# A hybrid decoder's step: products for 64 sample rows put on both column halves of TensorE's array, and cached keys taken from two samples in turn

## The reference, cut to what matters

```python
cq, ckv, kr, dq, dk, dv, iq, iw, ik = jnp.split(xn @ w_in, offs, axis=-1)   # 1024 x 1768
...
s = (jnp.einsum('bthc,bsc->bhts', ql, ckv).astype(jnp.float32)
     + jnp.einsum('bthr,bsr->bhts', qr, kr).astype(jnp.float32)) * scale    # MLA scores
...
s = jnp.einsum('btgnd,btkgd->btgnk', qg, kg).astype(jnp.float32) * DSA_HEAD_DIM ** -0.5
...
return jnp.concatenate([o_mla, o_dsa.reshape(b, t, DSA_HEADS * DSA_HEAD_DIM)], axis=-1) @ w_o
...
return jnp.einsum('bhtm,bmhd->bthd', p, v).reshape(b, t, X_HEADS * X_HEAD_DIM) @ wo_x
```

## Time and profile before

| | |
|---|---|
| median of 3 runs | 2436.02 us (2435.57 to 2438.84) |
| profiled execution, whole | 2440.92 us |
| profiled execution, span from first to last instruction | 2439.2 us |
| PE busy | 2232.2 us (92%) |
| DVE, POOL, ACT busy | 1606.9, 1041.5, 882.3 us |
| mean granted TensorE clock | 0.927 |

### The profile page before, as it was taken

One profiled execution on the slowest core, in us unless ns is written; L12 is line 12 of the kernel. 1 busy time (PEld: TensorE's weight loads), 2 busy tenths in 40 slices (PEclk: granted clock), 3 DMA queues, 4 the chain that ended last, 5 costly groups with the idle time before them and its releaser, 6 DMA issues.

```text
span 2439.2 us, 37526 instructions
## 1 busy us (share of the span) xinstructions
PE 2232.2 (92%) x12808; PEld 1809.7 (74%) x12808; DVE 1606.9 (66%) x3389; ACT 882.3 (36%) x1407; POOL 1041.5 (43%) x968
## 2 busy tenths in 40 slices
PE   6988789899778969969999995999999999999998
PEld 3534445366674549969999995888888888888886
DVE  1333986187112336888899982688878888888775
ACT  2115234122122222245555562343334333343343
POOL 1001003442110012207877725787878777773221
PEclk9988679899878669989999997999999999999999
DMA  5000001545434024148888877499998989999983
GB/s 194 10 9 18 1 4 49 155 138 166 132 139 164 1 90 163 44 147 231 221 227 241 235 239 263 161 327 357 341 357 319 342 323 349 330 327 332 327 281 116
DMA packets 240121, 479.95 MB, mean 197 GB/s; under 512 B 49249, under 2 KB 141794, under 8 KB 238562
## 3 DMA queue, kind: packets, MB, share of 16 engines
q1 hardware_dynamic: 161666, 314.60, 38.2%
q0 software_dynamic: 71680, 144.69, 18.3%
q10 hardware_dynamic: 6624, 18.88, 2.2%
HBM read 436.26 MB, written 41.80 MB: 196 GB/s over the span
## 4 chain that ended last, share of the span: by engine, by line
PE 51%; DVE 3%; DMA 2%; ACT 1%; issue 0%; POOL 0%; SPq 0%; POOLq 0%; ACTq 0%
PE psC L2216 30%; PE psC L2233 19%; PE psC L2204 2%; DMA rU<-in_peer_uT 1%; DVE Ul L2042 1%; ACT Uh L1962 0%; DVE gi L1392 0%; DMA gates<-gst 0%; DVE ohC L2058 0%; DVE gv L1389 0%; DVE cand L1396 0%; DVE wide L1455 0%; DVE ohI L2055 0%; SPq L1850 0%; POOL stD L1949 0%
## 5 line engine op out<-in xcount | busy, mean ns | idle before, releaser
L2216 PE MATMUL psC<-xh,Uh 128*128 128x256 f32 (+1 forms) x2048 | 611.5, 299 | 44.8 <-DVE Ul L2042 42.9
L2216 PE MATMUL psC<-xl,Uh 128*128 128x256 f32 (+1 forms) x2048 | 605.9, 296 | 0.0
L2216 PE MATMUL psC<-xh,Ul 128*128 128x256 f32 (+1 forms) x2048 | 605.4, 296 | 0.0
L2216 PEld LDWEIGHTS psC<-xh,Uh 128*128 128x128 f32 x2048 | 387.4, 189 | 57.8 <-issue 25.5
L1911 POOL DMA_INDIRECT ring<-in_peer_v,idxV x256 | 293.8, 1148 | 246.9 <-DVE h L2099 133.8
L2216 PEld LDWEIGHTS psC<-xh,Ul 128*128 128x128 f32 x2048 | 387.9, 189 | 5.8
L2216 PEld LDWEIGHTS psC<-xl,Uh 128*128 128x128 f32 x2048 | 387.3, 189 | 0.0
L2042 DVE TENSOR_TENSOR Ul<-rU,Uh 128x1024 fp32r<-128x1024 f32 x256 | 312.2, 1221 | 89.8 <-ACT Uh L1962 88.6
L1919 POOL DMA_INDIRECT aS<-acts,idxA x256 | 313.7, 1225 | 79.6 <-issue 77.7
L2099 DVE SCALAR_TENSOR_TENSOR h<-ring,wS,h 128x1024 f32<-128x1024 f32 x256 | 327.7, 1287 | 10.4 <-DMA ring<-in_peer_v,idxV 10.1
L1962 ACT ACTIVATE Uh<-rU 128x1024 fp32r<-128x1024 f32 x256 | 270.0, 1055 | 131.1 <-DMA rU<-in_peer_uT 128.2
(11 more groups left out here) (305 smaller groups left out, 3341.7 us busy)
## 6 DMA issues: line engine op xcount, KB each, us to landing
rU<-in_peer_uT SPq DMA_DIRECT2D x256, 512.0 KB, 5.1
rV<-in_peer_v SPq DMA_DIRECT2D x128, 512.0 KB, 5.4
gr<-gates SPq DMA_DIRECT2D x32, 640.0 KB, 7.6
arena<-in_poolM SPq DMA_DIRECT2D x128, 128.0 KB, 2.1
acts<-stage SPq DMA_DIRECT2D x32, 512.0 KB, 5.3
gates<-gst ACTq DMA_DIRECT2D x6, 2048.0 KB, 8.5
wraw<-in_w_pq SPq DMA_DIRECT2D x16, 512.0 KB, 3.5
gates<-zeros SPq DMA_DIRECT2D x4, 2048.0 KB, 8.8
```

What stands on the lines that cost most here:

```text
L2216: last = M(bank(6 + k, hi - lo), a[:, at, c], x[:, d, lo:hi], start=(d == 0 and a is Uh and x is xh), stop=(d == KD - 1 and x is xl))
```

## The change

Four products change, and nothing else.

1. For the 64 sample rows, the projection takes the ranges 0 and 1 together and then 2 and 3: for every `k`, one `M` for the even range into partitions 0 to 63 of its bank and one for the odd range into partitions 64 to 127 of its bank. Before the first `M` of a pair, PE waits until both banks of the block before are copied out.
2. `pair_scores` takes a page of sample 0 and a page of sample 1 in turn, where it took four pages of one and then four of the other.
3. W_o of the samples alternates the two column halves, the second on partitions 64 to 127.
4. Cross W_o does so for the sample block, after a wait for both additions of the block before.

DVE and ACT read the upper partitions where the result is there.

```diff
+        def proj_bank(t, c):
+            return bank(2 + c, PC, p1=P) if t < 4 else bank(2 + c, PC, p0=NS * (c % 2), p1=NS * (c % 2) + NS)
+        def rows_of_half(t, half):
+            return {"p0": 0, "p1": P} if t < 4 else {"p0": NS * half, "p1": NS * half + NS}
...
-                for c in range(4):
+                for cs in ((0,), (1,), (2,), (3,)) if t < 4 else ((0, 1), (2, 3)):
                     if t >= 1:
-                        pe.wait_ge(S["pj_act"] if c < 2 else S["pj_dve"], 2 * (t - 1) + c % 2 + 1)
+                        pe.wait_ge(S["pj_act"] if cs[0] < 2 else S["pj_dve"], 2 * (t - 1) + cs[-1] % 2 + 1)
                     for k in range(KD):
-                        last = M(bank(2 + c, PC, p1=R), xT[:, k, toks(t)], win[:, k, c * PC:(c + 1) * PC],
-                                 start=(k == 0), stop=(k == KD - 1))
-                    last.then_inc(S["pj_mm"], 1)
+                        for c in cs:
+                            last = M(proj_bank(t, c), xT[:, k, toks(t)], win[:, k, c * PC:(c + 1) * PC],
+                                     start=(k == 0), stop=(k == KD - 1), skip_group_check=True)
+                            if k == KD - 1:
+                                last.then_inc(S["pj_mm"], 1)
...
                 for kc in range(5):
                     n = 512 if kc < 4 else NS
-                    for b2 in range(2):
-                        b = 2 * p + b2
...
-                        for a in range(4 if kc < 4 else 1):
+                    for a in range(4 if kc < 4 else 1):
+                        for b2 in range(2):
+                            b = 2 * p + b2
...
-            for half in range(2):
-                for k in range(KD):
-                    last = M(bank(2 + half, p1=NS), xT[:, k, SEQ:NTOK], w_o[:, k, 512 * half:512 * half + 512],
-                             start=(k == 0), stop=(k == KD - 1))
-                last.then_inc(S["wo_mm"], 1)
+            for k in range(KD):
+                for half in range(2):
+                    last = M(bank(2 + half, **rows_of_half(4, half)), xT[:, k, SEQ:NTOK],
+                             w_o[:, k, 512 * half:512 * half + 512], start=(k == 0), stop=(k == KD - 1),
+                             skip_group_check=True)
...
-            for i in range(2 * NBLK):
-                t, half = divmod(i, 2)
-                R = rows(t)
-                if i >= 2:
-                    pe.wait_ge(S["hx_done"], i - 1)
+            for t in range(NBLK):
+                for halves in ((0,), (1,)) if t < 4 else ((0, 1),):
+                    if t >= 1:
+                        pe.wait_ge(S["hx_done"], 2 * (t - 1) + halves[-1] + 1)
```

More of the change, by code:

```diff
@@ L423, in _ @@
                     act.wait_ge(S["pj_mm"], 4 * t + c + 1)
-                    nc.scalar.activation(proj[0:R, t, c * PC:(c + 1) * PC], bank(2 + c, PC, p1=R), ACT.Copy)\
+                    nc.scalar.activation(proj[0:R, t, c * PC:(c + 1) * PC], proj_bank(t, c), ACT.Copy)\
                         .then_inc(S["pj_act"], 1)
@@ L613, in _ @@
                     dve.wait_ge(S["pj_mm"], 4 * t + c + 1)
-                    V.tensor_copy(proj[0:R, t, c * PC:(c + 1) * PC], bank(2 + c, PC, p1=R))\
+                    V.tensor_copy(proj[0:R, t, c * PC:(c + 1) * PC], proj_bank(t, c))\
                         .then_inc(S["pj_dve"], 1)
@@ L890, in _ @@
                 hs = h[0:NS, 4, 512 * half:512 * half + 512]
-                V.tensor_tensor(hs, bank(2 + half, p1=NS), hs, ALU.add).then_inc(S["h_done"], 1)
+                V.tensor_tensor(hs, bank(2 + half, **rows_of_half(4, half)), hs, ALU.add).then_inc(S["h_done"], 1)
             norm_gain("mem")
@@ L911, in _ @@
                 hs = h[0:R, t, 512 * half:512 * half + 512]
-                V.tensor_tensor(hs, bank(i % 2, p1=R), hs, ALU.add).then_inc(S["hx_done"], 1)
+                V.tensor_tensor(hs, bank(i % 2, **rows_of_half(t, half)), hs, ALU.add).then_inc(S["hx_done"], 1)
             dve.wait_ge(S["hx_done"], 2 * NBLK)
@@ L1195, in pair_scores @@
                     n = 512 if kc < 4 else NS
-                    for b2 in range(2):
-                        b = 2 * p + b2
[L1198 to L1201, removed]
-                        for a in range(4 if kc < 4 else 1):
+                    for a in range(4 if kc < 4 else 1):
+                        for b2 in range(2):
+                            b = 2 * p + b2
+                            if kind == 0:
+                                q = qlTs[:, b, :, :].rearrange("p h t -> p (h t)")
+                            else:
+                                q = bdq[:, b, :, :, :].rearrange("p g n t -> p (g n t)")
                             if kc < 4:
@@ L1298, in _ @@
             pe.wait_ge(S["wo_in"], 16)
-            for half in range(2):
-                for k in range(KD):
-                    last = M(bank(2 + half, p1=NS), xT[:, k, SEQ:NTOK], w_o[:, k, 512 * half:512 * half + 512],
-                             start=(k == 0), stop=(k == KD - 1))
-                last.then_inc(S["wo_mm"], 1)
+            for k in range(KD):
[3 more added lines that the diff above has]
+                             skip_group_check=True)
+                    if k == KD - 1:
+                        last.then_inc(S["wo_mm"], 1)
             norm_transpose("mem")
@@ L1332, in _ @@
             pe.wait_ge(S["at_oe"], n_self + n_cross)
-            for i in range(2 * NBLK):
-                t, half = divmod(i, 2)
-                R = rows(t)
-                if i >= 2:
-                    pe.wait_ge(S["hx_done"], i - 1)
[L1338 to L1341, removed]
+            for t in range(NBLK):
+                for halves in ((0,), (1,)) if t < 4 else ((0, 1),):
+                    if t >= 1:
+                        pe.wait_ge(S["hx_done"], 2 * (t - 1) + halves[-1] + 1)
+                    for c in range(2):
+                        for half in halves:
+                            last = M(bank(half, **rows_of_half(t, half)), oxT[:, c, toks(t)],
+                                     wox[:, c, 512 * half:512 * half + 512], start=(c == 0), stop=(c == 1),
+                                     skip_group_check=True)
+                            if c == 1:
+                                last.then_inc(S["ox_mm"], 1)
 SELECT_SEMS = """cst_in key_in sq_done ms_done rstd_done xs_done tp_done xf_done xh_done xl_done
```

## The result

In six runs beside six of the kernel before, the changed kernel takes 2417.66 us against 2437.09: a ratio of 0.9921, 95% interval 0.9900 to 0.9943. So it is 19.4 us faster, where 23.4 were forecast; 2417.66 lies in the range given, near its upper end. Six more runs later gave 2418.12 against 2437.74. The profiled execution after has a span of 2420.3 us, 18.9 less than before.

What follows compares the result with a forecast made beforehand. TensorE, busy 92% of the 2439.2 us span, was taken as the bound. Terms 11.5 + 13.9 - 2.1 + 0.1 = 23.4 us, off the median 2436.02, gave 2412.6; range 2405 to 2420.

Steps and rivals of the forecast that it cites:

- Projection, 11.5 us: Samples' projection: 64 records become 32 slots, 12.0 us saved, less 0.48 for waiting on ACT's second copy; net 11.5.
- The first rival: All changed products: issuing in turn leaves weight loads unhidden, one before each product; 17 us slower, 2453; chance 3%.
- Pairs, 13.9 us: Cached pairs' scores: blocks of 8 slots save 0.43 us each at full clock; 13.9 in all, 10 to 16.8.
- Pairs 1 to 3, forecast 5.2: Cached scores at full clock, 0.43 us saved per block; part of the 6.9 forecast for pairs 1 to 4.
- Pairs 4 to 7, forecast 6.9: Cached scores: pair 4 at full clock; pairs 5 to 7 save 5.2 us, each beginning at 1.2 GHz.
- Pair 0, forecast 1.8 saved: First cached pair: three blocks at 1.2 GHz save 2.6 us, 0.8 given back if the clock rises when it did before.
- That just fits: Pair 3's last page: there near 577.3, PE comes at 577.9; caps the first three pairs' gain at 5.8 us.
- more than 2 us: Sign at pair 3: the forecast would be wrong if this pair waited longer than that.
- the rival in which pages hold the pairs: Pairs 5 to 7's pages land no earlier, pair 3 waits a little: 5.2 + 1.7 us not gained; 2419.5; chance 10%.
- W_o, 2.1 us lost: Samples' W_o: gain hidden by the memory cache's transfer, next product starts at half clock; 0.3 gained to 3 lost.
- W_o is felt: Rival at samples' W_o: memory cache lands sooner, W_o gives some 7 us, PE does not cool; 2403.5; chance 5%.
- Cross W_o, 0.1 us gained: Cross W_o's sample block: 1.7 us less, about 1.0 lost waiting for additions, 0.6 for DVE's last two; 0.1 left.

Runs made afterwards that it cites:

- pairs_alone: Kernel before with only the new order of the cached products (pages of sample 0 and 1 in turn); 2424.50 us, ratio 0.9950 to the kernel before.
- wo_alone: Kernel before with only W_o of the samples changed to alternate halves; 2438.84 us, ratio 1.0007 to the kernel before.
- pages_apart: Changed kernel with GpSimd's and ACT's shares of pair 4's pages issued only after pair 3's pages land; 2417.41 us, ratio 0.9920 to the kernel before.
- after_again: The changed kernel once more, unaltered, beside others on one chip; 2418.12 us, ratio 0.9910 to the kernel before.
- wo_cache: Kernel before with the samples' W_o change and a separate semaphore for the cross attention's memory cache; 2429.84 us, ratio 0.9972 to the kernel before.
- proj_alone: Kernel before with only the projection's part of the change; 2425.70 us, ratio 0.9953 to the kernel before.

## Why the forecast was right, and what it mis-sized

*Projection, 11.5 us: right.* The column falls by 10.6 to 12.4 us in the eight kernels with this part on both halves, and back with the halves taken away. The wait for ACT's second copy grew from 0.77 us to 1.20. The first rival falls: 64 records with 64 loads on all rows take 12.09 us. The rule of the Trainium skill named there (page "TensorE: Matmul & The Clock Gate", section "Part 3: Packing small matmuls": a load overlaps a matmul in flight only in another row group) does not hold here either.

*Pairs, 13.9 us: right in the block, too high in the sum.* The block saves 0.49 us (1.51 to 1.02) where I had 0.43 (1.09 left), so counting 12 and 8 slots came close. The whole time of pairs_alone, 13.6 us, is what was forecast. By places, against the one trace of the kernel before and over the nine with the new order, the gain is 10.5 us in the mean (6.0 to 13.8):
- Pairs 1 to 3, forecast 5.2: their mean is 100.7 us against 105.3, 4.6 less, with the waits in it; the traces with short waits reach 5.8.
- Pairs 4 to 7, forecast 6.9: mean 107.5 against 114.2, 6.7 less. The waits before pairs 5 and 6 stayed as I said.
- **Pair 0, forecast 1.8 saved, is the term that failed.** Its mean is 42.1 us against 41.3: nothing saved. I assumed that the clock would rise "at the same time as now"; it rose after 17.0 us in the profiled execution, where pair 0 had spent 12.8 so before. One trace could not carry that assumption. In the five traces of the old order, four of them with the same program up to there, pair 0 took 35.3 to 41.3 us, 37.7 in the mean, of which 0 to 12.8 at 1.2 GHz; the one of the kernel before was the slowest. All nine traces of the new order have some 17 to 23 us at 1.2 GHz, pairs_alone with its old projection too. Against the mean of the old order pair 0 has become 4.4 us longer. The windows below are of wo_alone (old order), pages_apart and after_again.
- "That just fits" was near the truth and too narrow: I priced pair 3's pages and not the second half of W_o's weights. SP's 96 pages kept their pace (107.00 and 105.75 us from first to last issue in the two traces of the changed kernel, 106.28 before), but in the first of them the wait for the last page ended 4.2 us after that, not 2.1. With 2.01 us pair 3's wait stands on the line that I drew for being wrong ("more than 2 us"). A wait there costs its 0.3 to 2 us, and in the two traces of the changed kernel a further stretch at 1.2 GHz behind it (3.4 us in the window at 570.5).

```profile
469.10:482.10 13.00, 11.75 (x81) 7.62 (x82) 9.46 (x13) 0.00 (x0) 5.52 (x12) 1.00 0.67 209
459.20:476.10 16.90, 16.90 (x67) 8.68 (x66) 8.78 (x8) 0.00 (x0) 7.45 (x15) 0.50 0.52 159
457.70:481.40 23.70, 22.97 (x87) 12.13 (x88) 13.81 (x18) 2.27 (x3) 10.15 (x21) 0.50 0.54 165
```

Together the pairs gave 7.8 and 8.3 us in the two traces of the changed kernel, 6 us short, more than the 4 by which the whole forecast was off; over the nine traces the term is 3.4 us short. Of the rival in which pages hold the pairs, the small wait ahead of pair 3 came true (and its like at pair 2); that pairs 5 to 7 would gain nothing did not.

*W_o, 2.1 us lost: right.* The column rises from 50.2 to between 51.8 and 53.0 in the five kernels with this part and the old semaphore; without the part it scatters from 50.1 to 51.3. In the whole time wo_alone lies 1.6 us above the kernel before, which its interval does not tell from nothing. The idle stretch is 5.4 to 6.6 us, line 1324 takes 15.7 to 16.9 in place of 13.9, and wo_cache shows that the transfer alone hid the gain. "W_o is felt" fell.

*Cross W_o, 0.1 us gained: as forecast, by its rows; no run has this part alone.* It answers to the earlier trace rows; DVE's timeline after:

```profile
862.12 0.69 DVE L920 TENSOR_TENSOR h<-psA,h 128x512 f32<-128x512 f32 x1 [1.02 <-PE psA L1354]
864.84 1.41 DVE L920 TENSOR_TENSOR h<-psA,h 64x512 f32<-64x512 f32 x2 [2.02 <-PE psA L1354]
```

From the start of the last addition of 128 rows to the end of the two of 64 it takes 4.13 us (862.12 to 866.25), before 4.26 (881.14 to 885.40).

What stays open: why the clock stays down longer in pair 0 and, in two traces of fourteen, up through the index scores. The runs show that it differs between kernels with the same program up to there, and that the stretch in pair 0 was longer in every trace of the new order, not by what rule. It was not tried to keep it up in pair 0.

## What to carry to other kernels

Two products of 64 columns each, issued in turn onto the two halves, halve PE's time; where the products already overlap by half, as in the pairs (1.51 us where 1.95 would be in series and 1.02 came out), only the other half is left to win. Before shortening a stage, look for what ends with it: a transfer that lands as the product ends takes the whole gain, and the product behind the wait starts at the lower clock; one semaphore for three transfers was enough for that. Shortening a stage also moves everything behind it towards loads that keep their own pace, so price each load there, not the last one alone.

## What the runs showed of the hardware beyond that

Runs of the changed kernel spread by 12 to 16 us (2409.62 to 2425.71 in the first six), those of before by 3.3 (2435.57 to 2438.84 beside them), and the shorter ones go with a higher mean clock: 0.927 for 2409.62, 0.922 for 2422.01 and 2425.71. In two traces a wait of 1.45 us (pair 2 of proj_alone) and of 2.01 us (pair 3 of the changed kernel) was followed by some microseconds at 1.2 GHz.
